# Two-block hybrid transformer on one Trainium2 core: low parts of some weights from VectorE instead of GpSimd, second block's orders placed anew

## What is computed

```python
def hybrid_layer(x, mod, norm1, norm2, w_in, ..., w_out, w_ff1, w_ff2):
    shift1, scale1, gate1, shift2, scale2, gate2 = jnp.split(mod[:, None, :], 6, axis=-1)
    h = rms_norm(x, norm1) * (1.0 + scale1) + shift1
    proj = h @ w_in                      # 512 + 512 + 768 + 24 columns
    u, q, kv, gates = ...                # pool input, queries, keys and values, gates
    y_pool = pool_mixer(u, pool_w, pool_scale)
    y_nsa = nsa_mixer(q, kv[:, :, 0], kv[:, :, 1], gates, ...)
    mix = jnp.concatenate([y_pool, y_nsa], axis=-1) @ w_out
    x = x + gate1 * mix
    h2 = rms_norm(x, norm2) * (1.0 + scale2) + shift2
    ff = jnp.square(jax.nn.relu(h2 @ w_ff1)) @ w_ff2      # 1024 -> 4096 -> 1024
    return x + gate2 * ff

def second_block(x, c, w_mod, b_mod, ...):
    c_act = jax.nn.silu(c)
    for l in range(DEPTH):
        mod = c_act @ w_mod[l] + b_mod[l]
        x = hybrid_layer(x, mod, ...)
```

## Time and profile before

| | us |
|---|---|
| median of three runs | 2506.04 (2504.82 to 2506.50) |
| the profiled execution, own time | 2507.29 |
| its span, first to last instruction | 2505.5 |
| PE busy (matmuls and turns) | 2414.9 |
| DVE busy | 1365.2 |
| GpSimd busy | 1289.0 |
| ACT busy | 934.5 |
| mean granted TensorE clock | 0.994 |

### The profile page before, as it was taken

How to read it: one execution, slowest core, us unless ns; L and a number is a source line. 1 busy time by engine, 2 the same in 40 slices (tenths; PEclk the granted TensorE clock), 3 DMA queues, 4 the chain that set the end, 5 groups by cost and what they waited for, 6 DMA issues and landing times. The chain is left out here.

```text
span 2505.5 us, 36332 instructions
## 1 busy us (share of the span) xinstructions
PE 2414.9 (96%) x12167; PEld 1936.7 (77%) x12171; DVE 1365.2 (54%) x2819; ACT 934.5 (37%) x1691; POOL 1289.0 (51%) x2900
## 2 busy tenths in 40 slices
PE   6999999999999999999999998999999999899999
PEld 5777878788877777878888667777788856788887
DVE  5487453654448755355467646543658663522325
ACT  4433343432443334343244743222224473332221
POOL 4455644546545564454555214576774422555663
PEclk9999999999999999999999999999999999999999
DMA  5322423235422242323542112434543201232332
GB/s 167 92 68 84 145 92 109 93 97 177 154 86 72 81 152 92 118 76 102 179 121 64 43 34 77 167 125 146 177 139 96 74 27 41 81 99 92 102 108 78
DMA packets 132815, 258.26 MB, mean 103 GB/s; under 512 B 21994, under 2 KB 28700, under 8 KB 132636
## 3 DMA queue, kind: packets, MB, share of 16 engines
q1 hardware_dynamic: 132636, 255.94, 32.5%
HBM read 251.70 MB, written 4.21 MB: 102 GB/s over the span
## 5 line engine op out<-in xcount | busy, mean ns | idle before, releaser
L968 POOL TENSOR_TENSOR wl<-raw,wh 128x128 fp32r<-128x128 f32 (+2 forms) x2896 | 1288.8, 485 | 1191.1 <-ACT wh L1355 1190.6
L1037 PE MATMUL ps<-wh,hTh 128*128 128x512 f32 (+3 forms) x1600 | 633.0, 396 | 5.8 <-DVE hTl L2305 3.0
L1037 PE MATMUL ps<-wh,hTl 128*128 128x512 f32 (+3 forms) x1600 | 613.7, 384 | 0.0
L1037 PE MATMUL ps<-wl,hTh 128*128 128x512 f32 (+3 forms) x1600 | 612.7, 383 | 0.0
L1355 ACT ACTIVATE wh<-raw 128x1024 fp32r<-128x1024 f32 (+2 forms) x362 | 372.2, 1047 | 434.8 <-PE ps L1037 306.0
L1037 PEld LDWEIGHTS ps<-wh,hTh 128*128 128x128 f32 x1600 | 302.6, 189 | 77.7 <-issue 23.3
L1037 PEld LDWEIGHTS ps<-wh,hTl 128*128 128x128 f32 x1600 | 301.7, 189 | 57.4
L1037 PEld LDWEIGHTS ps<-wl,hTh 128*128 128x128 f32 x1600 | 302.7, 189 | 49.4
L1037 PE MATMUL ps<-hTh,wh 128*128 128x512 f32 (+2 forms) x704 | 260.9, 371 | 15.2 <-DVE hTl L1929 6.7
L1037 PE MATMUL ps<-hTh,wl 128*128 128x512 f32 (+2 forms) x704 | 258.8, 368 | 0.0
L1037 PE MATMUL ps<-hTl,wh 128*128 128x512 f32 (+2 forms) x704 | 258.8, 368 | 0.0
(11 more groups left out here) (274 smaller groups left out, 3136.1 us busy)
## 6 DMA issues: line engine op xcount, KB each, us to landing
raw<-in_w_in_dram SPq DMA_DIRECT2D x160, 512.0 KB, 3.6
raw<-in_w_ff_dram SPq DMA_DIRECT2D x128, 512.0 KB, 3.7
modw<-in_w_mod_dram SPq DMA_DIRECT2D x96, 512.0 KB, 4.7
raw<-in_w_br_dram SPq DMA_DIRECT2D x24, 512.0 KB, 3.7
raw<-in_w_out_dram SPq DMA_DIRECT2D x24, 512.0 KB, 3.8
xm<-in_x_dram SPq DMA_DIRECT2D x8, 512.0 KB, 4.7
raw<-in_w_out_dram SPq DMA_DIRECT2D x16, 256.0 KB, 3.8
raw<-in_w_in_dram SPq DMA_DIRECT2D x8, 408.0 KB, 3.3
```

What stands on the lines that cost most here:

```text
L968: last = pool.tensor_tensor(low[part], whole[part], high[part], ALU.subtract)
L1037: last = pe.matmul(*args, start=(q == 0 and c == 0 and n_pass == 0), stop=(q == u["quarters"] - 1 and c == u["chunks"] - 1 and n_pass == 2))
```

## The change

A function `on_vector` chooses the pieces of ek, ev, fu and fd, 72 of a layer of the second block, 144 of 368 in the whole program. Their low parts are made by DVE, in one instruction for a piece, as a step `low` of DVE's list; GpSimd leaves them out, and PE waits for them on DVE's semaphore. The other products' pieces (first block, eq, eu, mix) stay with GpSimd.

```diff
+LOW_LATER = 2
+def on_vector(u):
+    return u["name"][:2] in ('ek', 'ev', 'fu', 'fd') and (u["name"], u["l"]) != ("bq", 0)
...
-    return out, units
+    pieces = [(i, q) for i, u in enumerate(units) for q in range(u["quarters"])]
+    last = {(step[1], step[3]): n for n, step in enumerate(out) if step[0] == "sweep"}
+    swept = [n for n, step in enumerate(out) if step[0] == "sweep"]
+    lows = {}
+    for g, (i, q) in enumerate(pieces):
+        if on_vector(units[i]):
+            freed = max(last[piece] for piece in pieces[:g - SPLIT + 1])
+            lows.setdefault(swept[min(swept.index(freed) + LOW_LATER, len(swept) - 1)], []).append(("low", i, q))
+    return [x for n, step in enumerate(out) for x in [step] + lows.get(n, [])], units
...
             for g in range(G):
                 u = stream[g][0]
+                if on_vector(u):
+                    continue
                 pool.wait_ge(act_high, at("high", g))
...
-                pe.wait_ge(pool_low, at("low", g))
+                pe.wait_ge(dve_result if on_vector(u) else pool_low, at("low", g))
...
+                elif kind == "low":
+                    _, i, q = step
+                    u, g = units[i], start[i] + q
+                    dve.wait_ge(act_high, at("high", g))
+                    dve.tensor_tensor(piece(wl, g % RING, u), piece(raw, g % RING, u), piece(wh, g % SPLIT, u).bitcast(F32), ALU.subtract)\
+                        .then_inc(dve_result, mark(dve_result, ("low", g)))
```

A `low` step stands two sweeps behind the one that frees its buffer, unless MOVED moves it. The text SECOND and the second block's entries of MOVED are written anew for PE, ACT and DVE (most lines of the diff). SP's list of transfers follows the sweeps. The first block's sweeps and steps keep their order. Of SECOND, the end, around the last value product and the output product:

```diff
-pair_turn.3.1.3 mix0.1.0 pair_max.3.1.0 pair_prob.3.1.2 mix0.1.1 mix0.1.2/ pair_exp.3.1.2 pair_value.3.1
-pair_max.3.1.1 pair_max.3.1.2 mix0.1.2 mix0.1.3 mix1.0.0 pair_prob.3.1.3 mix1.0.1/ mix1.0.1 mix1.0.2/
+mix0.0.3 pair_turn.3.1.3 mix0.1.0 pair_prob.3.1.2 pair_max.3.1.0 mix0.1.1 mix1.0.0 mix0.1.2/ pair_value.3.1
+mix1.0.1/ mix1.0.1 mix0.1.2 mix1.0.2/ mix0.1.3 mix1.0.2 pair_prob.3.1.3 mix1.0.3/ mix1.0.3 pair_max.3.1.1
```

More of the change, by code:

```diff
@@ L172 @@
[L172 to L176, removed]
@@ L191, in steps @@
             out.append(("front" if word.endswith("/") else "sweep", named[kind], *rest))
-        elif kind == "evac":
+        elif kind in ("evac", "low"):
             out.append((kind, named[rest[0]], *rest[1:]))
@@ L343 @@
[L343 to L347, removed]
@@ L363 @@
[L363 to L366 removed]
+                  scale.a.0>gains low.ek.2>turn.a.0 turn.a.1>low.ek.2 low.ek.3>ek.0.1 stats.a.3>ek.0.2
@@ new lines @@
+                  scale.a.1>turn.a.3 low.ev.0>scale.a.1 ek.0.3>evac.ek.0 low.ev.1>ek.1.2/ low.ev.2>ev.0.1
+                  evac.ek.1>k_rot.1 low.ev.3>ev.0.2 evac.ev.0>pair_exp.0.0.2 evac.ev.1>cmp_turn.1
+                  eq.0.3>evac.eq.0 evac.eq.1>eq.0.3 evac.eu.0>eu.1.1 evac.eu.1>pair_logits.0.1.2
+                  scale.f.0>pool.1 stats.f.0>pair_max.2.1.1 scale.f.1>pair_exp.3.0.0
+                  evac.mix0.0>pair_max.3.0.2 low.fu0.0>mix1.0.2 stats.f.1>pair_prob.3.1.3 low.fu0.1>mix1.1.0
@@ new lines @@
+                  evac.mix0.1>low.fu0.1 pair_max.3.1.1>mix1.1.2 evac.mix1.0>turn.f.1 low.fu0.2>fu0.0.0
+                  stats.f.2>fu0.0.1 stats.f.3>stats.f.2 low.fu1.0>fu0.0.2 evac.mix1.1>fu0.1.0
+                  evac.fu0.0>fu0.1.1 fu0.0.3>evac.fu0.0 turn.f.2>fu0.0.3 pair_max.3.1.2>fu0.1.2
+                  turn.f.3>pair_max.3.1.2 low.fu1.1>evac.fu0.2 fu0.2.3>low.fu1.1 low.fu1.2>fu0.3.1
+                  fu1.1.0>fu1.0.0 evac.fu0.3>fu1.0.2 low.fd00.0>fu1.0.3 evac.fu1.0>fu1.1.1
+                  pair_max.3.1.3>fu1.1.2 evac.fu1.1>fd00.0.0 low.fd00.1>fd00.0.1 low.fd01.0>fd00.1.0
@@ new lines @@
+                  mix0.0.2>o_split.2 mix0.0.3>pair_turn.3.0.3 pair_exp.3.1.1>pair_exp.3.1.2
+                  pool.3>pair_exp.3.1.1 pair_turn.3.1.3>mix0.1.1 o_split.3>mix0.1.2 mix1.0.0>mix0.1.3
+                  stats.f.0>mix1.0.0 mix1.0.1>stats.f.1 mix1.0.2>mix1.0.1 scale.f.0>mix1.1.2 fu0.0.2>fu0.0.1
+                  fu0.0.3>stats.f.3 scale.f.1>fu0.0.3 evac.fu0.0>fu0.2.1 turn.f.3>evac.fu0.0
+                  evac.fu0.1>fu0.2.2 evac.fu0.2>fu0.3.1 evac.fu0.3>evac.fu0.2 evac.fu1.0>fu1.0.2
+                  fu1.1.0>fu1.0.3 fd00.0.0>evac.fu1.1 fd01.0.1>evac.fd00.1 fd01.1.0>fd01.0.1
@@ L516 @@
-                  mod.6.0>evac.bz.1 mod.5.0>evac.bz.1 mod.4.0>topk.2.1 mod.3.0>index.2.7 mod.2.0>index.0.7
-                  mod.1.0>evac.bq.0 mod.0.0>evac.bq.0 constants.0>evac.bq.0 scale.n.1@1>mod.31@0
-                  evac.fd70.1@0>scale.a.0@1"""}
+                  y_tok.c.3>y_turn.c.0 y_turn.c.3>evac.br20.0 low.ek.2>turn.a.1 low.ek.1>low.ek.2
+                  turn.a.3>scale.a.1 low.ev.0>evac.ek.0 evac.ek.1>low.ev.0 low.ev.2>evac.ek.1
+                  rstd.ek.0>low.ev.1 k_rot.0>rstd.ek.0 low.ev.3>k_rot.0 evac.ev.0>k_rot.2 cmp_in.0>k_rot.3
@@ new lines @@
+                  pair_max.3.1.2>pair_max.3.1.1 pool.3>pair_max.3.1.2 pair_max.3.1.3>pair_prob.3.1.1
+                  evac.mix0.0>pair_prob.3.1.3 o_split.3>evac.mix0.0 low.fu0.0>evac.mix1.0
+                  scale.f.0>low.fu0.0 low.fu0.1>scale.f.0 turn.f.1>low.fu0.2 low.fu0.3>evac.mix1.1
+                  scale.f.1>low.fu0.3 low.fu1.0>evac.fu0.1 evac.fu0.3>evac.fu0.2 evac.fu1.1>low.fd00.1
+                  low.fu2.0>low.fu2.1 low.fu2.2>low.fd10.0 evac.fu2.1>low.fd11.1 low.fu3.0>evac.fd10.1
```

233 lines of the change are left out of this document (121 added, 112 removed).

## The result

The changed kernel takes 2483.8 us (median of four runs, 2481.9 to 2486.4) against 2505.7 for the one before in the same rounds: a ratio of 0.9916, 95% interval 0.9903 to 0.9928. Timed once more on another occasion it was 2482.7 against 2502.2, 0.9924 (0.9911 to 0.9936). It is 19 to 22 us faster; 7.3 were forecast, and the range ended at 2489.

What follows compares the result with a forecast made beforehand. PE, busy 96%, was taken to bound the kernel, so only its 90.6 us idle counts. Terms +3.8, 0, -3.0, -7.1 and -1 sum to -7.3: 2500.0 profiled, 2498.8 median; forecast 2494 to 2503, outer range 2489 to 2510.

Steps and rivals of the forecast that it cites:

- DVE's prices: DVE's one low instruction per piece: 1.22 us in the feed-forward, 0.97 for ek, 1.02 for ev.
- End of the output product: Value product to mix0.1.2: work placed between covers a 1.5 us wait for L2305 in each layer, -3.0 us.
- Heads of the feed-forward: Start of both layers' feed-forward: GpSimd's waits go, but the norm's chain still ends the head; 0, ends -4.3 to +4.9.
- The body of the first feed-forward: Behind the feed-forward's head: 5.8 us idle goes; with other waits 9.1, less 2.0 given back, -7.1 for both layers.
- Input heads: Start of both layers: DVE lows delay the xm additions and the chain behind them, +1.9 us each, +3.8 together.
- I take 0: Input heads: no clock effect counted from splitting the pause, though some 1.5 us might return; ends widened 2 us a layer.
- Attention parts: Both layers' attention: the new order closes some small waits and tightens others; -1 us, ends -7 and +5.
- nothing in the trace prices another order: Attention parts: the trace was said to give no price for another order of the same steps; -1 us taken.
- (a): The new order also closes the attention parts' waits: -6 us more, 2492.8; chance 0.14.
- (b): Feed-forward: lows and evacuations queue on DVE behind `mod`s waiting for DMA, taking back the gain: 2504.4 to 2507.1; chance 0.19.
- (c): Attention parts: a GpSimd run holds DVE's low of ev.3, costing PE 9.8 us a layer: 2518.4, slower; chance 0.13.
- (d): Waits the trace puts down to GpSimd were truly a late ACT part or DMA: 2505.9; chance 0.07.

Runs made afterwards that it cites:

- the order alone: New order of every engine, but all low parts stay on GpSimd, against the kernel before: 2500.5 us against 2509.7, ratio 0.9958.
- the one-operand kernel: `mod` without its product with c_act, all low parts on GpSimd: span 2492.9 us in the old order, 2478.5 in the new.

## Why the prediction was off

**What held.** DVE's prices: 1.22 us forecast and 1.221 measured at 1024 elements, 0.97 and 0.952 at 768, 1.02 and 1.005 at 816:

```profile
L1880 DVE TENSOR_TENSOR wl<-raw,wh 128x1024 fp32r<-128x1024 f32 x128 | 153.1, 1221 | 65.9 <-ACT wh L1397 65.2
...
L1880 DVE TENSOR_TENSOR wl<-raw,wh 128x816 fp32r<-128x816 f32 x8 | 7.9, 1005 | 0.8 <-ACT wh L1397 0.7
L1880 DVE TENSOR_TENSOR wl<-raw,wh 128x768 fp32r<-128x768 f32 x8 | 7.4, 952 | 0.0
```

With GpSimd silent the 34 `mod`s of the feed-forward took 1.22, none more:

```profile
L2171 DVE SCALAR_TENSOR_TENSOR modw<-modw,cact x34: 1214/1219/1227, 1554.6 to 1868.8; 128x1024 f32<-128x1024 f32 x34
```

**End of the output product**, -3.0: right, 3.0 us when undone. **Heads of the feed-forward** with fu's waits behind them (0, and -1.1 and -1.0 out of the feed-forward's term): from the value product to fd00, less the 2.7 us of mix1.0.0 that now comes ahead of it, the layers lost 3.4 and 2.4 us, where the terms say 2.6 and 2.5. Right but for 0.8 us. (A sweep is 12 matmuls, 2.7 us, and its half 6; "24" and "12" above are wrong, and the sums, which use 2.7 us, do not hang on it.)

**The body of the first feed-forward**, -5.8 and -1.1 (the wait at 1581.71) and 2.0 given back, so -4.9: -3.9 between the first two profiles and -11.4 between the second two. That the first pair comes near the forecast is luck, and the cause was named half. Of the 5.8 us I gave 4.5 to GpSimd's pace because PE's list names it; with one operand they go while GpSimd keeps the work. What goes with them differs from one execution to the next: 318.1 and 323.3 us in two profiles before, 327.6 with the order alone, against 314.2, 311.9 and 314.5 in three of the changed kernel. What DVE's queue gives back was 3.0 us in the first profile (two waits for wl of 1.3 and 0.35, one for a bank of 1.1, one of 0.25), for 2.0 forecast.

**Input heads**, +3.8: a step that failed is "I take 0" for the clock. The turn did come later, as the sum says: 12.6 us behind ek's first sweep instead of 10.9, and 14.4 instead of 12.3. But the clock's lower stretch moved with the first pause from the turns onto sweeps with time to spare: two sweeps of 2.1 us stand between the pauses, not one of 2. Without the lows the heads are only 0.3 us shorter each, so the price of the lows was 0.3 and not 1.9. Set against the kernel before, PE's first five sweeps with the turns between them take 18.95 us for 18.5 in the first layer and 20.8 for 20.9 in the second, so +0.5 and -0.1. The prediction had this mechanism and its size ("some 1.5 us come back") and counted it as a bound instead of asking which of the two pauses the clock falls in. The earlier trace rows has the low clock behind a pause of 5.89 us; the first layer's head, which I did not use, has it behind one of 4.43, near the 4 us of the first part:

```profile
1293.18 3.22 PE L991 MATMUL ps<-cf,arena 128*128 128x128 f32 x16 [4.43 <-ACT arena L1481]
1293.00:1296.00 3.00, 2.82 (x16) 2.82 (x17) 1.82 (x3) 1.50 (x3) 2.02 (x6) 0.62 0.08 14
```

**Attention parts**, -1: the largest miss. PE's idle time went from 9.2 to 3.7 us in the first layer and from 6.2 to 3.7 in the second (-8.0, and -11 against the second profile of before, where the second layer had 9.2 too). From PE's sixth sweep of ek to the last value product, less the 2.7 us of mix1.0.0, the layers are shorter by 6.3 and 3.4 us, so -9.7; the 1.7 us beyond the idle time I cannot place. All of it is the order: with the order alone both layers have the changed kernel's lengths there within 0.2 us. The step that failed is "nothing in the trace prices another order". The list of PE's waits there names a step at each wait, and each could have been looked at: how many sweeps of 2.7 us stand between that step and the one it waits for, in the old order and in the new. For cmp_key it is half a sweep before and one and a half now, and the wait of 0.8 us at 1347.4 had to go; putting that one step back costs 2.8 us of wait in each layer. The same reading of the steps where PE waited before (cmp_hidden.0, q_rope.2 and q_rope.3, pool.1, the first turns of the last row tiles) might have given most of the 8 us; no run puts these back, so what each gave is not shown. I had looked for places that the new order makes tight and not for those that it makes loose.

**The first block**, nothing: 3.65 us of the difference of the first two profiles lie there and are chance; the runs' medians carry less of it.

Together, against the forecast of -7.3: 3.4 us less from the input heads, 8.7 from attention, 0.8 from the feed-forward's heads, 0.3 in the second feed-forward and 3.65 in the first block, with 1.0 us more in the first feed-forward's body, make -23.1; the spans differ by 23.0.

**Rivals.** (a) was nearest, attention's waits closed; with it the forecast was 2492.8, and the rest is the heads, a larger gain in attention, and chance. (b) was wrong: the `mod`s' waits for DMA were 22.9 us in the first feed-forward, longest 6.2, and even 15.2 us in the one-operand kernel cost PE nothing. (c) did not happen: ev's lows took 1.005 us, as GpSimd does nothing from the head to eq's first pieces. (d) is nearly what the runs show for the body: the waits that the trace puts down to GpSimd were not its pace; but their true cause, the hold, was removed by the same edit.

On the rule weighed there: both readings occur. In the kernel before 27 `mod`s start within a run of GpSimd that goes on for at least 1.75 us more, and are done in 1.21 to 1.56 us; beside them one GpSimd instruction takes some 1.44 us. That is the rule's way. Ten others took 1.8 to 11.4 us and ended with the run, which is the row's way and not the rule's. The Trainium skill's page "SBUF — State Buffer", section "Who interferes with whom", also says that a DVE instruction with at most one SBUF input, outside the two-port modes, does not contend with GpSimd. The trace agrees: with one operand none of the 33 `mod`s of the body took over 1.222 us.

## What to carry to other kernels

Where the engine that sets the time waits often for a short chain of other engines, read for each such wait how much of its own work lies between the two steps in the new order, and price the loosened places as carefully as the tightened ones. An idle row that names GpSimd's tile need not mean that GpSimd is slow: look for two-operand DVE instructions, or GpSimd instructions beside them, far over their usual time, and try the kernel with one operand less before moving the work. A pause in the middle of PE's spare work can be cheaper than the same pause at its end, as the slower clock behind it then falls on work that has time.

## What the runs showed of the hardware

A `mod`, a DVE instruction with two SBUF operands, that starts within a run of GpSimd subtractions has one of two fates. Either it gets in: it takes 1.21 to 1.56 us, and the GpSimd instruction beside it 1.44 for 0.46. Or it is held until the run is over and ends 1.08 us behind it, however long that is: 11.42 us beside 31 subtractions (the run ends at 1573.8, the `mod` at 1574.9) and 14.79 beside 48 (1682.9 and 1684.0). In the kernel before 27 got in and 10 were held, with the order alone 29 and 8. What decides between the two is not shown.

Nor is one operand always enough. In the kernel before a TENSOR_SCALAR that reads one tile is held twice in the first block:

```profile
22.00 6.18 DVE L1882 TENSOR_SCALAR nsm<-stat 128x2 f32<-128x2 f32 x1
310.44 5.97 DVE L2111 TENSOR_SCALAR arena<-arena,soft 128x128 f32<-128x128 f32 x1
```

L1882 takes 0.17 us in the second layer's head, and both of these end within 0.1 us of the end of a run of GpSimd subtractions. The one-operand `mod`, which writes an accumulator besides, never was: its 96 took 1.204 to 1.222 us.

PE's clock stood at 0.50 behind pauses of 4.8 and 6.1 us, and was low behind one of 3.8 (0.74 over the next 6.5 us, in which there is the pause of 0.49). Behind the same pause of 2.84 and 2.83 us in the two layers of the kernel with cmp_key put back it was 1.00 and 0.54: the length of the pause alone does not tell whether the clock falls.
